# Prompt attention on one core: who frees the closing banks, where combinations and maxima stand, and value products one pair behind their scores

## The reference, cut to what matters

```python
def nsa_block(q, qpos, gates, kc, vc, cmp_end, gather_sel, kw, vw, kw_pos, ns):
    s = jnp.einsum('bqgjd,bngd->bgjqn', qg, kc).astype(jnp.float32) * scale
    p = masked_softmax(s, cmp_end[None, :] <= qpos[:, None])
    o_cmp = jnp.einsum('bgjqn,bngd->bqgjd', p.astype(vc.dtype), vc)
    ...
    o_slc = jnp.einsum('bgjqk,bgqkd->bqgjd', p.astype(vs.dtype), vs)
    ...
    p = masked_softmax(s, (dist >= 0) & (dist < WINDOW) & (kw_pos[None, :] >= 0))
    o_win = jnp.einsum('bgjqk,bkgd->bqgjd', p.astype(vw.dtype), vw)
    g = jax.nn.sigmoid(gates.astype(jnp.float32)).reshape(b, tq, NSA_GROUPS, HPG, 3)
    o = g[..., 0:1] * o_cmp + g[..., 1:2] * o_slc + g[..., 2:3] * o_win
```

## Time and profile before

| what | value |
|---|---|
| median of 3 runs | 2638.7 us (2637.68 to 2643.01) |
| the profiled execution: its time | 2634.91 us |
| its span in the profile | 2633.1 us |
| busy share, whole span | TensorE 86%, VectorE 40%, ScalarE 21%, GpSimd 17% |
| mean granted clock of TensorE, whole span | 0.908 |
| instructions of TensorE in the stage (matmuls) | 1466 of 13162 |
| GpSimd's adds L1087 | 50, 118.4 us, 2368 ns each |

### The profile page before, as it was taken

How to read it: one execution, slowest core, us unless ns; L and a number is a source line. 1 busy time by engine, 2 the same in 40 slices (tenths; PEclk the granted TensorE clock), 3 DMA queues, 4 the chain that set the end, 5 groups by cost and what they waited for, 6 DMA issues and landing times. The chain is left out here.

```text
span 2633.1 us, 32958 instructions
## 1 busy us (share of the span) xinstructions
PE 2270.2 (86%) x13162; PEld 1924.0 (73%) x13162; DVE 1049.5 (40%) x1988; ACT 556.9 (21%) x986; POOL 450.1 (17%) x174
## 2 busy tenths in 40 slices
PE   5598896888886878887779999797999999999997
PEld 3477684333335757887668888796998989898996
DVE  1754074454532222455511111415443444344345
ACT  2476163333331101111111110103111101101110
POOL 0211010133441001110011100212222212211120
PEclk9798897888896578988889999898999999999998
DMA  7111253000003222110123322212211111111101
GB/s 277 45 44 55 52 189 118 1 1 0 1 0 136 93 89 71 50 41 27 42 76 101 103 68 84 99 30 53 65 49 33 49 49 43 39 49 49 33 33 66
DMA packets 135814, 164.57 MB, mean 63 GB/s; under 512 B 11058, under 2 KB 108083, under 8 KB 131108
## 3 DMA queue, kind: packets, MB, share of 16 engines
q1 hardware_dynamic: 125366, 109.85, 13.8%
q0 software_dynamic: 7552, 48.16, 5.5%
q10 hardware_dynamic: 2768, 4.70, 0.5%
HBM read 149.10 MB, written 17.87 MB: 63 GB/s over the span
## 5 line engine op out<-in xcount | busy, mean ns | idle before, releaser
L242 PE MATMUL psall<-hT,ring_short 128*128 128x344 f32 x1536 | 506.3, 330 | 64.0 <-POOL ring_short L237 41.4
L244 PE MATMUL psall<-hT,ring_short 128*128 128x344 f32 x1536 | 499.2, 325 | 0.0
L243 PE MATMUL psall<-work_short,ring_short 128*128 128x344 f32 x1296 | 420.1, 324 | 14.4 <-issue 14.4
L237 POOL TENSOR_TENSOR ring_short<-ring,ring_short 128x2048 fp32r<-128x2048 f32 (+3 forms) x49 | 197.7, 4035 | 1028.9 <-DVE ring_short L232 1028.8
L242 PEld LDWEIGHTS psall<-hT,ring_short 128*128 128x128 f32 x1536 | 296.8, 193 | 66.7 <-issue 36.6
L244 PEld LDWEIGHTS psall<-hT,ring_short 128*128 128x128 f32 x1536 | 296.6, 193 | 14.9 <-issue 14.9
L243 PEld LDWEIGHTS psall<-work_short,ring_short 128*128 128x128 f32 x1296 | 248.4, 192 | 0.6
L2652 DVE SCALAR_TENSOR_TENSOR xT<-psall,mod,xT 128x344 f32<-128x344 f32 (+1 forms) x264 | 151.4, 573 | 129.6 <-PE psall L244 126.5
L242 PE MATMUL psall<-work_short,work_short 128*128 128x344 f32 x480 | 161.2, 336 | 0.0
L1087 POOL TENSOR_TENSOR ring<-ring 128x1024 f32<-128x1024 f32 x50 | 118.4, 2368 | 248.0 <-ACT ring L1230 193.6
L243 PE MATMUL psall<-xT_short,ring_short 128*128 128x344 f32 x480 | 158.7, 331 | 0.0
(11 more groups left out here) (381 smaller groups left out, 4045.9 us busy)
## 6 DMA issues: line engine op xcount, KB each, us to landing
ring<-in_ada_w SPq DMA_DIRECT2D x24, 1024.0 KB, 6.5
ring<-in_w_up SPq DMA_DIRECT2D x44, 512.0 KB, 5.0
ring<-in_w_in SPq DMA_DIRECT2D x20, 512.0 KB, 3.9
work<-in_w_down SPq DMA_DIRECT2D x10, 1024.0 KB, 4.9
x_spill<-xT SPq DMA_DIRECT2D x1, 4128.0 KB, 17.2
xT<-x_spill SPq DMA_DIRECT2D x1, 4128.0 KB, 14.5
work<-in_x_prompt ACTq DMA_DIRECT2D x1, 4096.0 KB
work<-in_w_in SPq DMA_DIRECT2D x8, 512.0 KB, 5.2
```

The source lines that it names most:

```text
L237: return eng.tensor_tensor(lo, src, hi, ALU.subtract)
L242: pe.matmul(out, w[0], x[0], start=first, stop=False)
L243: pe.matmul(out, w[0], x[1], start=False, stop=False)
L244: return pe.matmul(out, w[1], x[0], start=False, stop=last)
```

## The change

It does six things: VectorE's first product of a combination reads the gate from SBUF, where ScalarE copies it (`gate`, for which the region `work` grows by 512 words); the logarithm is written to SBUF too and frees the bank (`logged` in place of `weighed`); ScalarE waits for the previous combination before this copy and no longer between logarithm and exponential; combinations wait until four banks after the closing in place of two (at the next closing as before); maxima are spread by costs (`cost`, `late`), at most about 1.3 of them for each pair, and a turn may not directly follow its own last maximum once pairs run; value products stand one pair behind their scores. Numbers of instructions are the same but for 24 copies on ScalarE.

```diff
@@ attention_order
-    due = [sum(1 for x in ahead if max(0, x[1].first - 2) <= i) for i in range(len(pairs))]
-    due = [max(n - 2 * j for j, n in enumerate(due[i:])) for i in range(len(pairs))]
+    cost = {"split": 0.0, "max": 1.0, "turn": 0.25}
+    late = {"split": 3, "max": 3, "turn": 1}
+    spent = [sum(cost[x[0]] for x in ahead[:n + 1]) for n in range(len(ahead))]
+    due = [sum(cost[x[0]] for x in ahead if max(0, x[1].first - late[x[0]]) <= i) for i in range(len(pairs))]
+    due = [max(n - 1.3 * j for j, n in enumerate(due[i:])) for i in range(len(pairs))]
...
-        while done < due[i]:
+        while done < len(ahead) and (spent[done] <= due[i] or ahead[done][1].first - late[ahead[done][0]] <= i):
...
-            if name == "turn" and w.index >= closed + 3:
+            if name == "turn" and (w.index >= closed + 3 or i and i < w.first and order[-1][:2] == ("max", w)):
                 break
...
-        if i >= 2:
-            w, kw = pairs[i - 2]
+        if i >= 1:
+            w, kw = pairs[i - 1]
             order.append(("values", w, kw))
...
-    for w, kw in pairs[-2:]:
+    for w, kw in pairs[-1:]:
@@ slot, close (TensorE)
-                        pe.wait_ge(weighed, w.index + 1)
+                        pe.wait_ge(logged, w.index + 1)
...
-                pe.matmul(out[:, 1, :], pick[:, 1, :], shift[b.index % 3], start=True, stop=True)
+                pe.matmul(out[:, 1, :], pick[:, 1, :], shift[b.index % 3], start=True, stop=True).then_inc(gated, 1)
@@ invert (ScalarE)
-                total = both[slot_of["close", b.index, 0] % 3][:, 0, :]
+                ps = both[slot_of["close", b.index, 0] % 3]
+                wait(act, combined, b.index)
+                act.wait_ge(gated, b.index + 1)
+                act.activation(gate, ps[:, 1, :], ACT.Copy)
                 act.wait_ge(summed, b.index + 1)
-                ch.link(act, act.activation(total, total, ACT.Ln, bias=tiny))
-                wait(act, combined, b.index)
-                act.activation(scaled, total, ACT.Exp, scale=-1.0).then_inc(rooted, 1)
+                act.activation(scaled, ps[:, 0, :], ACT.Ln, bias=tiny).then_inc(logged, 1)
+                act.wait_ge(logged, b.index + 1)
+                act.activation(scaled, scaled, ACT.Exp, scale=-1.0).then_inc(rooted, 1)
@@ combine (VectorE)
-                n = slot_of["close", b.index, 0] % 3
                 v.wait_ge(rooted, b.index + 1)
-                v.tensor_tensor(scaled, both[n][:, 1, :], scaled, ALU.mult).then_inc(weighed, 1)
+                ch.link(v, v.tensor_tensor(scaled, gate, scaled, ALU.mult))
                 v.wait_ge(pv, b.last + 1)
-                v.wait_ge(weighed, b.index + 1)
...
-                    while waiting and name in ("max", "turn") and slot_of["close", waiting[0].index, 0] + 2 <= n:
+                    while waiting and name in ("max", "turn") and slot_of["close", waiting[0].index, 0] + 4 <= n:
                         combine(waiting.pop(0))
```

More of the change, by code:

```diff
@@ L158, in allocate @@
     s.ring, s.ring_short = region("ring", 8192)
-    s.work, s.work_short = region("work", 25904)
+    s.work, s.work_short = region("work", 26416)
     s.ident = sb("ident", [P, P], F32)
@@ L1041, in stage_prompt_attention @@
     gate_hi = s.work_short(25840, NG, HPG)
-    scaled = view(s.work, 25032, 512)
+    scaled, gate = view(s.work, 25032, 512), view(s.work, 25904, 512)
     cmp_add = view(s.work, 25544, 256).bitcast(BF16).rearrange("p (t n) -> p t n", t=TT)
@@ L1056, in stage_prompt_attention @@
     added, summed, rooted = s.sem("a_added"), s.sem("a_summed"), s.sem("a_rooted")
-    weighed, combined = s.sem("a_weighed"), s.sem("a_combined")
+    gated, logged, combined = s.sem("a_gated"), s.sem("a_logged"), s.sem("a_combined")
     branches, order = attention_order()
@@ L1278, in list_rows @@
                 m, r = most[b.index % 2], rows[b.index % 2]
-                gate = s.gates[:, b.t, :].rearrange("p (g j c) -> p g j c", g=NG, c=3)[:, :, :, b.kind]
+                raw = s.gates[:, b.t, :].rearrange("p (g j c) -> p g j c", g=NG, c=3)[:, :, :, b.kind]
                 wait(v, turned, b.index - 1)
-                ch.link(v, high(v, gate_hi, gate))
+                ch.link(v, high(v, gate_hi, raw))
                 v.tensor_copy(r[:, :, 4:8], gate_hi)
-                low(v, r[:, :, 8:12], gate, gate_hi)
+                low(v, r[:, :, 8:12], raw, gate_hi)
                 v.wait_ge(maxed, units_of[b.index] + len(b.maxima))
```

## The result

The changed kernel takes 2609.95 us (median; 2607.06 to 2614.03), the kernel before 2639.52 on the same footing: ratio 0.9888, 95% interval 0.987 to 0.9905. The forecast was 2613 us. The profiled execution took 2609.34 us against 2634.91, 25.6 less. The stage alone went from 352.3 us (446.24 to 798.54) to 327.8 (448.31 to 776.07), 24.5 less, so all but a microsecond of the gain is there.

A forecast was written before the change was run, and what follows sets the result against it. TensorE, idle 54 us and lengthened about 36 us by half clock, was taken to bound the attention stage. Terms -14 (a), -8 (b), +4 (c), +1 (e), -9 (f) gave -26 us: from 2638.7 to 2613 us, range 2594 to 2634.

The forecast's parts named there:

- the core: Prompt attention stage: TensorE's idle time, 54 us, had to fall below 40 us, else the prediction's central claim was wrong.
- (a): Turns kept apart from their last maximum, maxima spread: 14 us gained, with 0.8 us left at each of ten turns.
- (b): Closing banks freed by ScalarE instead of VectorE: of 15.3 us of TensorE waits 7 remain, 8 gained.
- (c): ScalarE's 24 gate copies and longer double closings hold up value products: 4 us lost (0 to 15).
- (d): Combinations deferred to four slots after the closing: VectorE no longer stands before maxima; price counted in (a).
- (e): Value products one pair behind: the last branch's closing waits for GpSimd's add, 1 us lost.
- (f): TensorE's clock in the stage: fewer half-clock stretches start with shorter stalls, 9 us gained (0 to 20).
- B: VectorE's new product of two SBUF operands contends with GpSimd; half of (a) and (f) lost: 2624 us, chance 0.17.
- A: At seven double closings ScalarE's queue holds up value products: slower, 2652 us, chance 0.09.
- C: TensorE still idles about a microsecond at many places and half-clock time stays: 2622 us, chance 0.14.
- D: Turns and single closings nearly free of stall, most of the clock regained: 2596 us, chance 0.15.
- E: Double closings set the pace and VectorE still comes late, so nothing moves: 2636 us, chance 0.07.

The follow-up runs named there:

- banks_alone: Kernel before, with only ScalarE copying the gate after the previous combination and its logarithm freeing the closing bank; list unchanged: 2648.3 us, ratio 1.0045.
- values_two: Changed kernel with value products two pairs behind their scores instead of one: 2591.9 us, ratio 0.9843 to the kernel before.
- small-add runs: Kernel before, order_alone and changed kernel, each with GpSimd adding 8 of 512 columns per group: 2626.9, 2590.1 and 2582.1 us.
- order_alone: Kernel before with only the changed list: turn rule, spread maxima, value products one pair behind; VectorE still frees banks: 2594.0 us, ratio 0.983.
- turn_apart: Kernel before with only the rule that a turn may not directly follow its own last maximum: 2597.6 us, ratio 0.9852.
- combine_two: Changed kernel with combinations two banks behind the closing instead of four: 2605.7 us, ratio 0.988 to the kernel before.

## Why the prediction was right or wrong

The time was right, 2613 against 2610, but in part by luck: the sum's parts were off against each other. By TensorE's waits the turns gave 11 us less than forecast, the banks 5 more, ScalarE took 1.5 less and the clock gave 2 more. Two of the signs failed: turns were to wait 14 us and waited 25.5, and the clock was to be 0.90 or more and was 0.89. The sign for the core, idle time below 40 us, was met by a hair: 39.9.

- **(a) turns, 14 us gained: wrong.** Measured after 533.2 us: 22.3 to 19.4, 2.9 gained. The rule itself was under-rated: alone, with early combinations, it takes all 22.3 away. The step that failed is the residue of 0.8 us a turn. I saw that the deferred combination stands before the last maximum, and priced it at 2.1 us; it takes 4.8 in the case shown, and six turns wait 3.2 us each.
- **(b) banks, 8 gained: the wait, yes, the gain, no.** All 15.3 us of waits for VectorE went and 2.2 for ScalarE came, 13.1 less where 8 were forecast. But three comparisons give the part a cost: +4.1 us on the kernel before, +8.9 with the turn rule, +9.7 with the whole list. (With value products two behind it gains, together with the deferral: 328.3 to 312.3.) Copy 0.60, logarithm 0.69 and exponential 0.63 us were priced within 0.03. That the wait for the previous combination now precedes all three was seen, but mis-sized: 1.2 us of stall were walked for a second closing, and banks_alone shows 3.14, behind a first product that an add had stretched to 1.64.
- **(c) ScalarE, 4 lost: 2.5.** TensorE's waits for the combination rose from 2.4 to 2.7 us. The two early stalls behind a query cut rose from 1.7 to 2.4 and from 2.9 to 4.4 us, the second by the 1.5 that was walked for each.
- **(d) deferral at nothing** beyond its share of (a): 3.7 us lost by one execution each, which isn't clear of the noise, and 7.7 against combining at the turn. In the timeline above it is what stands before the late turn.
- **(e) 1 lost: right for the end only.** The last closing waits 1.5 us for GpSimd, from 0.6. But in the changed kernel value products one behind are 15.5 us slower than two behind (values_two), which the prediction didn't see: of the closings that come a pair earlier it asked only whether their adds are done.
- **(f) clock, 9 gained: right,** 10.8. The long turn waits still cost it: behind one of 3.30 us that ended at 590.36 the changed kernel runs at half speed to about 599:

```profile
590.36 0.47 PE L1143 MATMUL psall<-ident,work 128*128 128x128 f32 x1 [3.30 <-DVE work L1293]
...
592.76 1.97 PE L1184 MATMUL psall<-ring,work 128*64 128x512 f32 x4
```

- **Rivals.** B was the true mechanism of what is missing. I gave it 0.17 and a loss of 11 us; 13.4 is what the two parts that expose the adds cost. It didn't show in the total because the turn rule was worth more than I took it for. The sign I had set for it, a mean of the SBUF product well over 1 us, was met just so: 26.5 us for 24, 1.10. A, C, D and E didn't come. (Value products wait 1.7 us for exponentials, where A set over 10.) The Trainium skill's statement (GPSIMD Engine Reference, Specifications) that GpSimd's SBUF interfaces are shared with VectorE is borne out by the stretched rows, 2.90 us for an add of 512 columns.

What stays open: which of the stretched steps costs how much in each arrangement (the small-add runs remove them all at once), what the bank part and the deferral are each worth without contention, and why two behind gains in one case and loses in the other, beyond where its closings fall. Double buffers for the gate and the reciprocal, which would free ScalarE from the previous combination, weren't tried.

**A better version** is among the runs: `order_alone` (2594.0 us, 0.983) beats both kernels. `turn_apart` (0.9852, one line) and `values_two` (2591.9) are no different from it by their intervals.

## What to carry to other kernels

Put one unit of other work between a producer's last step and the in-order consumer that needs its result: here a single line of list order gave 36 us of stage, more than the whole change. When a step is moved off one engine to save it time, look for what then precedes it on the new one, and try each part alone: here a total that came out as forecast hid two parts that cost 13 us. Before changing a product's operand from PSUM to SBUF, or moving small VectorE steps, look at what GpSimd runs at that moment.

## What the runs showed of the hardware that was not expected

- A VectorE step with only SBUF operands that begins during an add of GpSimd (two SBUF operands, 2.37 us) doesn't share the time with it but ends after it. In the changed kernel all 14 steps of 512 columns that did so ended 0.55 us (0.547 to 0.554) after the add, at lengths of 1.10 to 2.90 us instead of 0.69, and 8 casts of 8 columns ended 0.03 us after it, the longest of 1.93 us instead of 0.16 (2.33 in the case shown for combine_two). So the price is what is left of the add when the step begins, not a share of the step. VectorE's steps with an operand in PSUM aren't touched: the first products of the kernel before keep 0.69 us in all 24 cases, 7 of them during an add.
- The other way round, an add of GpSimd that begins while such a product runs is lengthened, from 2.37 to as much as 2.66 us in the changed kernel.
- For ScalarE on 512 columns the side matters little: logarithm into PSUM 0.662 us, into SBUF 0.687; exponential from PSUM 0.597, from SBUF 0.631. The Trainium skill (ScalarE: Activation LUTs, Step-by-step: what each stage is for) calls PSUM the faster destination; the rows of the logarithm agree, by 0.025 us.
- Waits at such places cost more than their own length. All six turn stalls of 3.1 to 3.3 us of the changed kernel were followed by a stretch at 1.2 GHz (value products of 1.97 us instead of 1.08 in the case shown). Of the turn stalls of 1.95 to 3.12 us of the kernel before, some were (3.12 at 560.05) and some not (2.36 at 636.43). 19.3 us of idle time less brought 16.9 us of busy time less in turn_apart.
